# Expert loop of a mixture-of-experts layer: weight units split five ahead, one activation-table load per block, silu moved by one unit

## What is computed

```python
a = jax.nn.silu(h @ lp['w_gate'][e]) * (h @ lp['w_up'][e])
y = y + combine[..., e, None] * (a @ lp['w_down'][e])
```

## Time and profile before

| what | value |
|---|---|
| three runs | 1992.34, 1995.51, 1996.05 us; median 1995.51 |
| profiled execution | 1997.25 us, its span 1995.7 us |
| mean granted TensorE clock | 0.941 |
| busy, share of the span | PE 90%, DVE 61%, ACT 46% |
| the expert loop | 1608 to 1964 us of the span |

### The profile page before, as it was taken

One profiled execution on the slowest core, in us unless ns is written; L12 is line 12 of the kernel. 1 busy time (PEld: TensorE's weight loads), 2 busy tenths in 40 slices (PEclk: granted clock), 3 DMA queues, 4 the chain that ended last, 5 costly groups with the idle time before them and its releaser, 6 DMA issues. The chain is left out here.

```text
span 1995.7 us, 25431 instructions
## 1 busy us (share of the span) xinstructions
PE 1800.4 (90%) x9097; PEld 1497.0 (75%) x9097; DVE 1214.3 (61%) x2156; ACT 918.9 (46%) x1456; POOL 118.1 (6%) x134
## 2 busy tenths in 40 slices
PE   7997899999998987889999999799968789999993
PEld 6876788888887765778888888687667778888872
DVE  3554668887224547357866522645573678888885
ACT  2446433232223436443233311433462479898884
POOL 1000000000000000001100000200000210101001
PEclk8998899999998998989999999699989689999996
DMA  4223224545332214125654333320212389999993
GB/s 146 85 74 112 85 64 138 148 138 147 106 95 74 60 57 169 43 60 156 177 157 138 106 100 99 94 85 1 65 43 65 117 309 365 378 353 363 351 350 137
DMA packets 203998, 289.83 MB, mean 145 GB/s; under 512 B 12348, under 2 KB 150564, under 8 KB 203780
## 3 DMA queue, kind: packets, MB, share of 16 engines
q1 hardware_dynamic: 188932, 240.08, 36.8%
q0 software_dynamic: 11920, 36.48, 6.0%
q10 hardware_dynamic: 3056, 12.06, 1.6%
HBM read 271.77 MB, written 22.05 MB: 147 GB/s over the span
## 5 line engine op out<-in xcount | busy, mean ns | idle before, releaser
L227 DVE TENSOR_TENSOR weights_low<-ring,weights_high 128x1024 fp32r<-128x1024 f32 x202 | 246.7, 1223 | 403.6 <-ACT weights_high L221 403.6
L200 PE MATMUL bank<-XH,weights_high 128*128 128x512 f32 x1120 | 454.0, 405 | 34.5 <-DVE XL L69 20.3
L202 PE MATMUL bank<-XH,weights_low 128*128 128x512 f32 x1120 | 444.5, 397 | 0.0
L201 PE MATMUL bank<-XL,weights_high 128*128 128x512 f32 x1120 | 443.8, 396 | 0.0
L221 ACT CAST weights_high<-ring 128x1024 fp32r<-128x1024 f32 x202 | 211.2, 1047 | 438.5 <-PE bank L202 436.7
L200 PEld LDWEIGHTS bank<-XH,weights_high 128*128 128x128 f32 x1120 | 215.5, 192 | 83.1 <-ACT squares L69 12.3
L202 PEld LDWEIGHTS bank<-XH,weights_low 128*128 128x128 f32 x1120 | 214.8, 192 | 46.7
L201 PEld LDWEIGHTS bank<-XL,weights_high 128*128 128x128 f32 x1120 | 215.4, 192 | 43.0 <-issue 0.5
L2150 DVE TENSOR_TENSOR XL<-ring,XH 128x1024 fp32r<-128x1024 f32 x144 | 171.3, 1221 | 31.7 <-ACT XH L2144 31.7
L2144 ACT CAST XH<-ring 128x1024 fp32r<-128x1024 f32 x144 | 145.6, 1049 | 0.2
L69 DVE SCALAR_TENSOR_TENSOR squares<-ring,c_silu,squares 128x128 f32<-128x128 f32 x384 | 135.1, 352 | 13.6
(11 more groups left out here) (481 smaller groups left out, 3112.2 us busy)
## 6 DMA issues: line engine op xcount, KB each, us to landing
ring<-in_w_ffn_in SPq DMA_DIRECT2D x88, 512.0 KB, 4.8
ring<-in_w_gate SPq DMA_DIRECT2D x72, 512.0 KB, 5.5
ring<-in_w_up SPq DMA_DIRECT2D x72, 512.0 KB, 7.3
ring<-in_w_down SPq DMA_DIRECT2D x72, 512.0 KB, 6.3
ring<-in_w_ada POOLq DMA_DIRECT2D x48, 512.0 KB, 4.7
ring<-in_w_ffn_out SPq DMA_DIRECT2D x44, 512.0 KB, 3.5
ring<-in_w_out SPq DMA_DIRECT2D x24, 512.0 KB, 3.6
slot_output<-expert_out SPq DMA_DIRECT2D x19, 512.0 KB, 6.9
```

The lines of the kernel that those rows point to most:

```text
L200: PE.matmul(out_ap, w_h, x_h, start=first, stop=False, skip_group_check=True)
L201: PE.matmul(out_ap, w_h, x_l, start=False, stop=False, skip_group_check=True)
L202: return PE.matmul(out_ap, w_l, x_h, start=False, stop=last, skip_group_check=True)
L227: V.tensor_tensor(wl[:, s, :], ring[s][:, :], wh[:, s, :].bitcast(F32), ALU.subtract).then_inc(split_done.sem, 1)
```

## The change

Four edits. `AHEAD` goes from 4 to 5: the prologue splits units 0 to 4, and in every place of a block the unit split is one further on. The one-element silu that brings the table is issued at the head of the block. Silu of the gate product stands behind `split_ahead(3)` as before, but now those are units 5 to 8, and unit 9 is `split_ahead(4)`. At the end of a block the units split run from 11 over 0 to 4 of the next block, and the next block's gathered rows stand behind the same units as before (11 and 0).

```diff
-HELD, AHEAD = 6, 4
+HELD, AHEAD = 6, 5
...
             reach(PE, l_silu, b)
+            reach(S, l_table, b)
+            S.activation(table_in[:, :], ones[0:1, 0:1], ACT.Silu).then_inc(l_table.sem, 1)
             for q in range(4):
                 split_ahead(q)
                 if q == 2:
                     reach(PE, l_hgl, b * 2 + 2)
                 gate(q)
-            split_ahead(4)
-            reach(S, l_table, b)
-            S.activation(table_in[:, :], ones[0:1, 0:1], ACT.Silu).then_inc(l_table.sem, 1)
             reach(S, l_used, b * UNITS + 4)
             reach(S, l_av, b * 2)
             S.activation(sg[:, :], bank[0][:, :], ACT.Silu).then_inc(l_silu.sem, 1)
             reach(PE, l_av, b * 2)
-            split_ahead(5)
+            split_ahead(4)
             unit_high(b, 10)
...
-            for q in range(7, UNITS):
+            for q in range(6, UNITS):
                 split_ahead(q)
-                if q < 9 and not last:
-                    split_rows(b + 1, q - 7)
+                if q in (6, 7) and not last:
+                    split_rows(b + 1, q - 6)
```

## The result

The changed kernel takes 1978.88 us (median of four runs, 1978.50 to 1979.64) against 1995.78 us before (1992.34 to 1998.56): ratio 0.9917, 95% interval 0.9899 to 0.9934. The forecast was 1978.3 us.

A forecast was written before the change was run, and what follows sets the result against it. A ring of waits among ScalarE, VectorE and TensorE was taken to bound the expert loop. Closing TensorE's holes, 15.3 + 17 x 0.11 = 17.2 us, from 1995.51 gave 1978.3 us, range 1975.1 to 1984.

The forecast's parts named there:

- The mechanism: Expert-loop block: ScalarE's load and silu run late, delaying VectorE's unit 9, `hidden(0)` and TensorE's turn; a 0.97 us hole.
- Part 1, the load: ScalarE in each expert-loop block: one table load instead of two, taking away 1.3 us, with no drain seen.
- Part 2, five ahead: Unit 4's cast (0.95 us) and low part (1.14 us) move one block earlier; no work added, prologue cost taken as 0.
- The sum: TensorE's idle time at the turn of the hidden rows: 15.3 us plus 17 x 0.11, a gain of 17.2 us.
- the clock: Granted clock in the expert loop: expected to stay 1.00, given no share; below that, none of the sums would hold.
- One sign: Expected sign in the expert loop: ScalarE idles 0.9 us longer before the turn of the hidden rows.
- Rival A: DMA takes over in the expert loop: 375 GB/s ends the gain once 6.4 us reserve is gone; 1989.1 us, chance 0.08.
- B: Something on ScalarE 0.7 us late makes `hidden(0)` 0.55 late per block, half the hole stays; 1987.6 us, chance 0.05.
- C: Nothing measurable: the second table load is needed after all, or the hole has another cause; 1995.5 us, chance 0.04.
- D: Slower: unit 4's cast, before the `expert_out` copies, waits for its landing and delays later fetches; 2000 us and up, chance 0.03.
- the ring: Expert-loop bound: ScalarE's backlog delays VectorE's unit 9, `hidden(0)` and TensorE's turn, which ScalarE awaits; period 19.47 us.

The follow-up runs named there:

- e1: Changed kernel with the one-element silu back right before silu of the gate product, so two table loads per block, still five ahead; 1995.24 us, ratio to before 0.9998.
- e2: Changed kernel with `AHEAD` left at 4, keeping one table load at the block's head; 1981.61 us, ratio to before 0.9913.
- e6: Changed kernel with one more 512 KB fetch per block, into a tile nobody reads; 1979.37 us, loop 338.52 us.
- e4: Changed kernel with one more 128x512 copy on ScalarE at each block's head, result unused; 1987.15 us, ratio to before 0.9950.

## Why the prediction was right, point by point

- **The mechanism** held in each step: load, silu, unit 9, `hidden(0)`, turn. The worked times in the new block were silu 7.79 us (7.78 measured), unit 9's cast 8.27 (8.27), `hidden(0)` 10.91 (10.87), period 18.45 (18.45), VectorE's slack 0.16 us (0.12).
- **Part 1, the load**, is shown to carry the gain, by e1 and e2. The 1.30 us start to start were right, and no drain appeared. What was missed is small: a load also starts 1.07 us behind a cast (1694.87 to 1695.94 before), where the next cast starts after 0.95, so the one in the middle cost 0.12 us more, 1.42 in all. The worked times had this right all the same, since they put 0.95 there. Of this the period got 1.02 per block, because TensorE's own work then bounds.
- **Part 2, five ahead**, I had costed at nothing and it is worth about 0.04 us per block (e2). In the prologue it was hidden, as said: from the first turn of gathered rows to gate unit 0 it is 3.70 us before (1604.85 to 1608.55) and 3.71 after (1601.49 to 1605.20).
- **The sum.** Term 17.2 us; the holes fell from 20.18 to 3.24, by 16.94. That step was right to 0.3.
- **What the sum lacked** is the clock behind the exit, 1.6 us against the change: the loop became 15.6 us shorter (353.91 to 338.30), not 17.2. I had written that I gave the clock no share of its own. The median fell by 16.9 all the same. The other 1.3 us must come from outside the loop; the part ahead of it scatters by more than that (in the two profiles it is 3.35 us shorter after the change), but which part gave them in these runs isn't shown. So the 0.6 us between forecast and median are in part luck.
- **One sign** was worked out wrong: ScalarE was to idle 0.9 us longer before the turn. It idles 1.57 us instead of 1.17, 0.4 longer, and the prediction's own table gives that too (end at 10.2, the copy behind the turn at 11.8).
- **Rival A** was priced too near: its 393 GB/s is no ceiling, but the DMA fell behind at 414 (e6), 5% above what the changed kernel asks for. Its reserve of 6.4 us is 6.5 to 7.1 in the changed kernel. **B** did not come, and e4 shows that its price rule, lateness beyond the slack times 17, holds. **C** fell with e1 and e2. **D** needed landings to slip by 6.4 us; with 7% more to move 5.2 us of the reserve went, and no cast waited.

## What to carry to other kernels

When several engines are each busy for nine tenths, follow one block from start to start and look for the ring; what leaves the ring's sum is gain, what is only moved along it is not. A table load at a loop's head and one in its middle can be made one by asking for the needed table first, since the plain casts ran alike behind it. And look at how a loop ends: five iterations skipped by a condition cost 2 us here and the clock 1.6 more, and a loop end in a register cost nothing that showed. Where fetches run ahead, follow the time from landing to use over the blocks: a loop that loses nothing can still be eating its reserve.

## What the runs showed of the hardware that I had not expected

- The granted clock fell to 0.50 for 3.4 us behind a gap of 2.17 to 3.49 us in all six profiles that have such a gap and periods of 18.33 to 18.54 us, and in none of the three with 18.84 or 19.47 us and gaps of 2.17 to 2.25 us. Why the faster kernels pay it and the slower ones don't stays open.
- The DMA engines moved 375 GB/s at a busy share of 0.99, 408 over 275 us at 1.02, and fell behind at 414 and 1.03: the busy share says little of what is left.
- Two skipped loop iterations left no gap on TensorE, five left 2.2 us.
